# A dense two-block transformer kernel on one core: the opening's transfer of c, the squares of x and their sum, and the order of root and modulation rows

## The reference

```python
def rms_norm(x, w):
    xf = x.astype(jnp.float32)
    y = xf * lax.rsqrt(jnp.mean(xf * xf, axis=-1, keepdims=True) + EPS)
    return (y * w.astype(jnp.float32)).astype(x.dtype)

def modulate(x, w, shift, scale):
    return rms_norm(x, w) * (1 + scale[:, None, :]) + shift[:, None, :]
...
    c_act = jax.nn.silu(c)
    mod = (jnp.einsum('bd,dn->bn', c_act, w_ada[l]) + b_ada[l]).reshape(b, N_SUB, 3, D_MODEL)
    h = modulate(x, norm_w[l, 0], mod[:, 0, 0], mod[:, 0, 1])
    x = x + 0.5 * mod[:, 0, 2][:, None, :] * swiglu(h, ffn_w13[l, 0], ffn_w2[l, 0])
```

## Time and profile before

| what | value |
|---|---|
| runs shown | 1014.84, 1015.24, 1017.86 us (median 1015.24) |
| profiled execution | 1014.84 us, its span 1013.1 us |
| mean granted TensorE clock | 0.997 |
| busy share of the span | PE 97%, PEld 91%, DVE 77%, ACT 53%, POOL 1% |
| SyncE issues, start | c 0.72, constants 1.13, columns 1.53, unit 0 at 2.00 |
| ScalarE's first square of each half of x | 5.26 and 6.98 us |
| first matmul of the loop over k | 18.04 us |

### The profile page before, as it was taken

How to read it: one execution, slowest core, us unless ns; L and a number is a source line. 1 busy time by engine, 2 the same in 40 slices (tenths; PEclk the granted TensorE clock), 3 DMA queues, 4 the chain that set the end, 5 groups by cost and what they waited for, 6 DMA issues and landing times.

```text
span 1013.1 us, 17325 instructions
## 1 busy us (share of the span) xinstructions
PE 983.3 (97%) x7016; PEld 917.8 (91%) x7016; DVE 776.2 (77%) x1423; ACT 536.2 (53%) x937; POOL 12.5 (1%) x32
## 2 busy tenths in 40 slices
PE   5999999999898999999999999999999999999996
PEld 4999998999897999999998988789999988988895
DVE  6999998979976887685776588556778877577665
ACT  5455554436576555453555545664555655355453
POOL 0000000004000000000000000000000000000000
PEclk9999999999999999999999999999999999999999
DMA  8996999855572655678664535364454555555531
GB/s 334 352 345 268 350 344 341 298 205 209 177 276 93 213 200 174 240 240 209 246 241 174 191 135 208 125 182 136 141 186 168 196 173 203 196 178 173 181 105 41
DMA packets 33277, 213.92 MB, mean 211 GB/s; under 512 B 3757, under 2 KB 6189, under 8 KB 8494
## 3 DMA queue, kind: packets, MB, share of 16 engines
q1 hardware_dynamic: 32910, 211.78, 59.5%
q10 hardware_dynamic: 288, 1.05, 0.3%
HBM read 210.19 MB, written 2.62 MB: 210 GB/s over the span
## 4 chain that ended last, share of the span: by engine, by line
PE 89%; DVE 6%; ACT 3%; issue 1%; DMA 1%; DVEq 0%; ACTq 0%
PE bank L216 87%; PE bank L219 2%; DVE sb_ring L195 1%; ACT sb_tmp L192 1%; ACT sb_ring L192 1%; ACT R L192 1%; DVE sb_tq L195 1%; DVE sb_tmp L195 1%; DVE sb_junk L204 1%; DMA sb_raw<-wts 0%; DMA sb_x<-xt 0%; DVE sb_acc L195 0%; DVE sb_st_v L207 0%; DVE sb_tmp L198 0%; DVE sb_nst L195 0%
## 5 line engine op out<-in xcount | busy, mean ns | idle before, releaser
L216 PE MATMUL bank<-sb_h,sb_ring 128*128 128x258 f32 (+2 forms) x3776 | 496.4, 292 | 6.7 <-DVE sb_h L201 3.9
L216 PEld LDWEIGHTS bank<-sb_h,sb_ring 128*128 128x128 f32 x3776 | 475.7, 190 | 20.9 <-issue 5.7
L195 DVE TENSOR_TENSOR sb_ring<-sb_raw,sb_ring 128x1024 fp32r<-128x1024 f32 (+1 forms) x324 | 385.2, 1205 | 2.8 <-ACT sb_ring L192 2.8
L192 ACT ACTIVATE sb_ring<-sb_raw 128x1024 fp32r<-128x1024 f32 (+1 forms) x324 | 320.4, 1038 | 79.3 <-DMA sb_raw<-wts 47.1
L216 PE MATMUL bank<-R_512r,sb_ring 128*128 128x256 f32 (+1 forms) x1608 | 225.3, 301 | 0.0
L216 PEld LDWEIGHTS bank<-R_512r,sb_ring 128*128 128x128 f32 x1608 | 211.3, 188 | 11.9 <-issue 0.3
L216 PE MATMUL bank<-sb_ring,sb_h 128*128 128x512 f32 (+1 forms) x504 | 112.5, 378 | 0.0
L216 PEld LDWEIGHTS bank<-sb_ring,sb_h 128*128 128x128 f32 x504 | 87.4, 188 | 16.6
L204 DVE CUSTOM_DVE_ANT_0 sb_junk<-sb_raw,sb_csil,sb_cols 128x1024 bf16<-128x1024 f32 x72 | 92.3, 1282 | 1.8
L216 PE MATMUL bank<-R_1024r,sb_ring 128*128 128x512 f32 (+1 forms) x576 | 91.6, 320 | 0.0
L216 PEld LDWEIGHTS bank<-R_1024r,sb_ring 128*128 128x128 f32 x576 | 82.0, 188 | 8.2
(11 more groups left out here) (158 smaller groups left out, 558.1 us busy)
## 6 DMA issues: line engine op xcount, KB each, us to landing
sb_raw<-wts SPq DMA_DIRECT2D x193, 1024.0 KB, 4.9
sb_raw<-wts SPq DMA_DIRECT2D x3, 512.0 KB, 3.9
scratch<-R SPq DMA_DIRECT2D x1, 1536.0 KB
sb_x<-xt ACTq DMA_DIRECT2D x2, 512.0 KB, 5.2
out<-R SPq DMA_DIRECT2D x2, 512.0 KB, 2.6
R<-scratch SPq DMA_DIRECT2D x2, 508.0 KB, 8.9
sb_raw<-wts SPq DMA_DIRECT2D x1, 768.0 KB, 4.5
sb_raw<-wts SPq DMA_DIRECT2D x1, 640.0 KB, 4.0
```

Of the source, the lines that this page charges most:

```text
L192: return Issued(self.e and self.e.activation(o, i, func, **kw))
L195: return Issued(self.e and self.e.tensor_tensor(*a))
L216: return Issued(self.e and self.e.matmul(o, w, m, start=start, stop=stop, skip_group_check=True))
```

## The change

c's transfer goes to all 128 partitions, straight into `csil`, and ScalarE applies Silu there to 128 x 1024; `spread_c` and the two copies are gone. ScalarE squares the even tiles of x and VectorE the odd ones; Silu stands between ScalarE's second and third square. VectorE adds the squares of tiles 5 and 7 (`two_squares_0`), and TensorE sums seven tiles over partitions and tiles at once (`sum_0`, in the order 1, 0, 3, 2, 5, 4, 6). The first unit's modulation rows are queued ahead of `token_factor` instead of behind the diagonals.

```diff
--- before.py
+++ after.py
@@ -19,6 +19,8 @@
 RK = 58
 BIG = 3.0e38
 LATE = 2
+
+SUM_ORDER = (1, 0, 3, 2, 5, 4, 6)
 Z_SCALE = -256.0 / 3.0
 PI_BELOW = float(np.nextafter(np.float32(np.pi), np.float32(0)))
 SCALE_1 = 96.0 ** -0.5
@@ -582,19 +584,21 @@
     def token_factor(self, st, on_pool=False):
         bank = self.m.banks[7].take()
         self.add("token_sums", st, bank, self.last_square)
-        if self.last_square:
-            done(self.last_square, ("sums", st))
+        done(self.last_square, ("sums", st))
         self.add("token_factor", st, bank, on_pool)
         return bank
 
     def x_norm(self, st, on_pool=False):
         bank = self.token_factor(st, on_pool)
+        return st, bank, self.diagonals(st, on_pool)
+
+    def diagonals(self, st, on_pool):
         diag = []
         for i in range(2):
             g = self.m.tq.take()
             self.add("diagonal", st, i, g, on_pool)
             diag.append(g)
-        return st, bank, diag
+        return diag
 
     def norm_rows(self, norm, func=FN.Copy):
         st, bank, diag = norm
@@ -676,24 +680,21 @@
         self.add("load_x")
         self.add("load_c")
         self.add("load_con")
-        self.add("silu_c")
-        cb = [B[i].take() for i in range(2)]
-        for i in range(2):
-            self.add("spread_c", i, cb[i])
         for _ in range(NR):
             self.load()
         self.add("load_rows")
         for f in range(NF):
+            if f == 4:
+                self.add("silu_c")
             self.add("square_0", f)
-            if f:
-                self.add("sum_squares_0", f)
-        for i in range(2):
-            self.add("csil", i, cb[i])
-            done(cb[i], ("csil", i))
-        self.last_square = None
-        norm = self.x_norm("f1")
+        self.add("two_squares_0")
+        bank = B[7].take()
+        for n, f in enumerate(SUM_ORDER):
+            self.add("sum_0", n, f, bank)
         self.take_unit()
         self.flush()
+        self.add("token_factor", "f1", bank, False)
+        norm = "f1", bank, self.diagonals("f1", False)
         self.take_unit()
         self.norm_rows(norm)
         bk = [b.take() for b in B]
@@ -1335,7 +1336,7 @@
 
     def load_c(self):
         m, e = self.m, self.e
-        e.dma_start(m.reg(52, 1024)[0:1, :], m.c_in[0:1, :]).then_inc(*self.up("c_in", ("c",), by=16))
+        e.dma_start(m.csil, m.c_in[0:1, :].to_broadcast([128, 1024])).then_inc(*self.up("c_in", ("c",), by=16))
 
     def load_con(self):
         m, e = self.m, self.e
...
@@ -1481,24 +1482,24 @@
         e.matmul(o.rearrange("p (s n) -> p s n", s=2), w[0], x, start, stop)
         self.went(e.matmul(o[:, 0:T], w[1], x[:, 0, :], False, stop), 128, *events)
 
-    def spread_c(self, i, bank):
-        m, e = self.m, self.e
-        e.wait_ge(*self.at("silu_c"))
-        e.wait_ge(*self.at("con"))
-        c = m.reg(52, 1024)[0:1, 512 * i:512 * i + 512]
-        e.matmul(bank.ap, m.ones[0:1, :], c, True, True).then_inc(*self.up("c_spread", ("spread_c", i)))
+    def sum_0(self, n, f, bank):
+        m, e = self.m, self.e
+        if n == 0:
+            self.turn(bank)
+            e.wait_ge(*self.at("con"))
+        e.wait_ge(*(self.at("two_squares_0") if f == 5 else self.at("square", "f1", f)))
+        sq = m.reg(36 + f, 256)
+        for i in range(2):
+            ins = e.matmul(bank.ap[:, 256 + 2 * i:258 + 2 * i], sq[:, 128 * i:128 * (i + 1)], m.ones[:, 0:2],
+                           n + i == 0, n == len(SUM_ORDER) - 1)
+        if n == len(SUM_ORDER) - 1:
+            ins.then_inc(*self.up("token_sums", ("sums", "f1")))
 
     def token_sums(self, st, bank, sq):
         m, e = self.m, self.e
         self.turn(bank)
         b = bank.ap
-        e.wait_ge(*self.at("acc", st, NF - 2 if sq else NF - 1))
-        if not sq:
-            for i in range(2):
-                ins = e.matmul(b[:, 256 + 2 * i:258 + 2 * i], m.acc[:, 128 * i:128 * (i + 1)], m.ones[:, 0:2], i == 0,
-                               True)
-            ins.then_inc(*self.up("token_sums", ("sums", st)))
-            return
+        e.wait_ge(*self.at("acc", st, NF - 2))
         for i in range(2):
             e.matmul(b[:, 256 + 2 * i:258 + 2 * i], m.acc[:, 128 * i:128 * (i + 1)], m.ones[:, 0:2], i == 0, False)
         e.wait_ge(*self.at("square", st, 7))
...
@@ -1922,19 +1923,15 @@
 
     def silu_c(self):
         m, e = self.m, self.e
-        c = m.reg(52, 1024)[0:1, :]
         e.wait_ge(*self.at("c"))
-        e.activation(c, c, FN.Silu).then_inc(*self.up("c_silu", ("silu_c",)))
-
-    def csil(self, i, bank):
-        m, e = self.m, self.e
-        e.wait_ge(*self.at("spread_c", i))
-        e.activation(m.csil[:, 512 * i:512 * i + 512], bank.ap).then_inc(*self.up("c_silu", ("csil", i)))
+        e.activation(m.csil, m.csil, FN.Silu).then_inc(*self.up("c_silu", ("silu_c",)))
 
     def square_0(self, f):
         m, e = self.m, self.e
-        e.wait_ge(*self.at("x_in", f // 4))
-        e.activation(m.reg(36 + f, 256), m.x[:, f, :], FN.Square).then_inc(*self.up("squares", ("square", "f1", f)))
+        if f % 2 == 0:
+            e.wait_ge(*self.at("x_in", f // 4))
+            e.activation(m.reg(36 + f, 256), m.x[:, f, :], FN.Square).then_inc(
+                *self.up("squares", ("square", "f1", f)))
 
     def square(self, st, f, b, permuted):
         m, e = self.m, self.e
...
@@ -2401,8 +2398,7 @@
     def ada(self, i, b, n):
         m, e = self.m, self.e
         e.wait_ge(*self.at("unit", i))
-        e.wait_ge(*self.at("csil", 0))
-        e.wait_ge(*self.at("csil", 1))
+        e.wait_ge(*self.at("silu_c"))
         e.wait_ge(*self.at("cols"))
         if self.junk_done:
             e.wait_ge(*self.junk_done)
@@ -2417,13 +2413,19 @@
         e.tensor_tensor(m.ring[:, w % NS, 1, a:b], m.raw[:, i % NR, a:b], m.ring[:, w % NS, 0, a:b].bitcast(F32),
                         ALU.subtract).then_inc(*self.up("weights_lo", ("lo", w, p)))
 
-    def sum_squares_0(self, f):
-        m, e = self.m, self.e
-        e.wait_ge(*self.at("square", "f1", f))
-        if f > 1:
-            e.wait_ge(*self.at("acc", "f1", f - 1))
-        e.tensor_tensor(m.acc, m.acc if f > 1 else m.reg(36, 256), m.reg(36 + f, 256), ALU.add).then_inc(
-            *self.up("squares_summed", ("acc", "f1", f)))
+    def square_0(self, f):
+        m, e = self.m, self.e
+        if f % 2:
+            x = m.x[:, f, :]
+            e.wait_ge(*self.at("x_in", f // 4))
+            e.tensor_tensor(m.reg(36 + f, 256), x, x, ALU.mult).then_inc(
+                *self.up("squares_here", ("square", "f1", f)))
+
+    def two_squares_0(self):
+        m, e = self.m, self.e
+        e.wait_ge(*self.last())
+        e.tensor_tensor(m.reg(41, 256), m.reg(41, 256), m.reg(43, 256), ALU.add).then_inc(
+            *self.up("squares_here", ("two_squares_0",)))
 
     def sum_squares(self, st, f, b):
         m, e = self.m, self.e
```

More of the change, by code:

```diff
@@ L1429, in run @@
     def run(self):
-        steps = {"spread_c": self.spread_c, "token_sums": self.token_sums, "spread": self.spread, "up": self.up_tile,
+        steps = {"sum_0": self.sum_0, "token_sums": self.token_sums, "spread": self.spread, "up": self.up_tile,
                  "up2": self.up2, "down": self.down, "down_1": self.down_1, "down_2": self.down_2,
@@ L1886, in run @@
     def run(self):
-        steps = {"hi": self.hi, "load_x": self.load_x, "silu_c": self.silu_c, "csil": self.csil, "square_0": self.square_0, "rbc": self.rbc, "h_hi": self.h_hi,
+        steps = {"hi": self.hi, "load_x": self.load_x, "silu_c": self.silu_c, "square_0": self.square_0, "rbc": self.rbc, "h_hi": self.h_hi,
                  "silu": self.silu, "hid_hi": self.hid_hi, "rope_sin": self.rope_sin, "hx_hi": self.hx_hi,
@@ L2372, in run @@
     def run(self):
-        steps = {"ada": self.ada, "lo": self.lo, "sum_squares_0": self.sum_squares_0, "sum_squares": self.sum_squares,
+        steps = {"ada": self.ada, "lo": self.lo, "square_0": self.square_0, "two_squares_0": self.two_squares_0, "sum_squares": self.sum_squares,
                  "token_factor": self.token_factor, "diagonal": self.diagonal, "acol": self.acol, "xr": self.xr,
```

## The result

The changed kernel took 1019.04 us (median of 20 runs, 1017.31 to 1020.71), the kernel before, run beside it, 1017.13 us (20 runs, 1014.65 to 1017.98). The ratio is 1.0021 with a 95% interval of 1.0014 to 1.0028: slower by about 2.1 us (1.4 to 2.8). That is less than the 0.3% set down ahead, but the interval leaves no doubt about the direction. The profiled execution took 1017.42 us, its span 1015.6, against 1014.84 and 1013.1.

A forecast was written before the change was run, and what follows sets the result against it. The start of xr, which moves VectorE's k loop and then TensorE, was taken as the bound. Sums and modulation rows ending at 13.8 plus 3.9 put it at 17.7, 1.8 later: 1017.0 us, range 1014.6 to 1018.8.

The forecast's parts named there:

- xr: First product of x with row scale and token factor, on VectorE ahead of the k loop; start 17.7 against 15.93.
- the footing: Total time: forecast put on the median of three runs of before, 1015.24, instead of the profiled 1014.84, giving 1017.0.
- The forecast shift of 1.8 us: Opening: xr starts at 17.7 instead of 15.93, and the whole loop and TensorE's end move with it.
- Rival B: Head of SP's queue: broadcast at 139 GB/s costs 3.77 us, xr at 20.0, all 4.0 later, 1019.3; chance 0.10.
- The term that was mis-sized: Head of SP's queue: sending c to 128 partitions costs 1.5 us, making constants land about 7.1, unit 0 11.1.
- x late by 0 to 1.5 us: Opening transfers: x may lose engines to c; the sum holds either way, as TensorE waits for constants at 7.1.
- Squares and table load hidden: ScalarE's opening: squares done by 10.4 despite a second table load of 1.28; TensorE wants the last at about 12.9.
- 28 passes, 6.5 us: TensorE's token sums: seven tiles, 14 matmuls, 0.2325 us per pass, 6.5 us, from 7.2 to 13.8.
- rival A: Opening: TensorE sums at the later, faster pace and c costs at most 1.23 us; level, 1015.5 to 1016.1; chance 0.27.
- Sums and modulation rows meet at 13.8: Ahead of the root: TensorE's sums and VectorE's modulation rows, started by unit 0 at 11.1, both end at 13.8.
- 3.9 us from the sums to xr, 1.3 us of it idle: Root, diagonals, factor spread and copy take 3.9 us before xr; VectorE idles some 1.3 us waiting for the copy.
- TensorE's end moves one for one with xr: After the k loop: from 60 us TensorE carries the chain, so xr's shift should be found again at 62 us.

The follow-up runs named there:

- The repeats: Kernel before and changed kernel, both unedited, each profiled a second time: 1016.63 and 1019.22 us.
- The run with 128 rows: Changed kernel, but c laid out in HBM as 128 equal rows, one per partition: 1017.61 us, ratio 1.0011 against the kernel before.
- split-ones: Kernel before with one modulation row each side of the root and c's spread using ones from a GpSimd memset: 1015.83 us, ratio 0.999; again 1014.88 us, 0.9987.

## Why the prediction was right or wrong

It was right in the direction and in the chain of waits that moves xr, and wrong in the time: 1019.04 lies above the range, whose end was 1018.8. Two steps of the sum were off.

**The step that failed** is the last one of the sum, the footing: "1015.24; on that footing 1017.0". Three runs of before stood for the kernel; in twenty its median is 1017.13, 1.9 us higher, which is nearly the whole distance from 1017.0 to 1019.04. The forecast shift of 1.8 us put on that median gives 1018.9. The range's upper side had room for a dearer transfer (1018.0) and 0.8 us beyond it, and none was set aside for the scatter of the runs, although the three shown already spread over 3 us. Later sets of 24, 24 and 15 runs of the same kernel had medians of 1016.20, 1016.13 and 1016.58, so even the median of a set moves by 1 us. The repeats show part of that scatter: the same kernel with or without the fall of the clock near 310 us.

That the totals differ by 2.1 us (1.4 to 2.8), close to the forecast's 1.8, is luck: xr moved by 2.8. In the profiles the shift is there up to 209 us, and no run shows where the missing 0.7 us goes. Rival B's 1019.3 is near the measured time by luck as well, since it stood on the same low footing and wanted xr at 20.0.

**The term that was mis-sized** is c's transfer: "1.5 us" between 1.23 and 2.5. It measured 2.2 us at x, 2.3 at unit 0 (9.6 to 11.9) and 3.1 at the constants (5.6 to 8.7). The run with 128 rows splits it. The bytes alone cost 1.3 us at unit 0, near the low end of 1.23, but 1.9 at the constants; the reading of one row added 1.0 and 1.1. So the sum's 1.5 left out most of the broadcast's own price, although the later broadcast row, 2.5 us for the same kind of transfer, was the nearer one, and it took one figure for every place, where the constants lost more. Why the bytes cost them more is open; all transfers together moved only 224 to 274 GB/s from 2 to 5 us, against the 426 of the sum. The consequence: TensorE's sums started at 8.73 instead of 7.2, took 6.15 us instead of 6.6 and ended at 14.9 instead of 13.8, and xr is 2.8 us late instead of 1.8.

Point by point:

- *x late by 0 to 1.5 us.* It came 2.2 late. c and x landed within 0.2 us of each other. The rule of queues taken in turn (the Trainium skill, "DMA: Bandwidth & Descriptors", SWDGE vs HWDGE vs iDMA) had put it 1.2 to 1.5 us late; the trace agrees that it comes late, and not with the size.
- *Squares and table load hidden.* Right: ScalarE's squares ended at 11.2, TensorE at 14.9. The second table load ran from 8.24 to 9.52 behind a square that ended at 8.22, and Silu started at 9.54: 1.3 us for the switch. The Trainium skill ("ScalarE: Activation LUTs", What ACT_TABLE_LOAD costs) puts it at 2.66 us with a drain; this trace does not agree.
- *28 passes, 6.5 us.* 6.15 us, 0.22 each. They did not become faster on the way, as rival A's mechanism wanted: six or seven passes fall into every microsecond from 9 to 14. The rule that activity releases an idle TensorE from half rate (the Trainium skill, "TensorE: Matmul & The Clock Gate", What's actually happening) does not show in these rows, whose granted clock reads 1.00 from the start.
- *Sums and modulation rows meet at 13.8.* They met, at 14.9 and 14.5.
- *3.9 us from the sums to xr, 1.3 us of it idle.* The sums ended at 14.88 and xr started at 18.76, 3.9 us later; VectorE idled 1.5 of it.
- *TensorE's end moves one for one with xr.* Shown at 62 us in all profiles; up to the mask's load at 209 us the distance to the loop's end is 148.9 to 149.1 us in all twelve of them. Behind it the scatter is as large as the effects.
- *Rival B* named the right place, the broadcast at the head of SP's queue, and a cost beyond 2.8 us at unit 0 as its turning point. The constants passed that, unit 0 did not.

## What to carry to other kernels

A large transfer issued first can delay every queue, not only its own: here 512 KB on SP's queue made x, on ScalarE's, 2.2 us late. Size it at each transfer behind it (2.3 us at unit 0, 3.1 at the constants), and price the reading of one row for all partitions by a row of the same kind. Do not send one row to all partitions by DMA where an idle TensorE can spread it beside other work, as it did here. An engine's queue gains when its waits are filled with pieces of the right size: here one modulation row on each side of the root brought xr forward by 0.4 us, and a constant that came by memset instead of by transfer by another 0.8. For effects of 0.2%, compare a landmark in the trace as well as totals, and give the median of a few runs a range as wide as those runs.

## What the hardware showed that I had not expected

- 512 KB sent to 128 partitions from one HBM row landed 6.6 us after its issue (c, in the change), and 5.4 us after it from 128 rows of their own. x, on the other queue, landed 1.1 us later beside the one-row transfer.
- TensorE's granted clock fell near 310 us in eight of twelve profiles, by no rule that these runs show: the kernel before, the change and split-ones each showed both. What decides it stays open, and so does why the falls between 260 and 270 us do not show in the time of the stretch.
- Fourteen f32 matmuls with two columns each, 6.15 us of unbroken work, kept the slow pass of 0.22 us to the end, where four such passes take 0.59 us later, while the granted clock reads 1.00 all along. In these profiles the recorded clock is no guide to TensorE's pace in the opening.
